# Output gates in the middle of the next chunk step, gate keys last, one rotation behind the levels

## The reference, cut to what matters

```python
def _hg_gates(hf, lb):                      # hf: forget columns, lb: learned lower bound
    logf = jnp.logaddexp(jnp.log(lb), jnp.log1p(-lb) + jax.nn.log_sigmoid(hf))
    return logf, -jnp.expm1(logf)           # log forget gate, key of the HGRN2 heads

def _merge(o_r, g_r, o_h, g_h, o_s, hg_norm_w, w_out, dtype):
    ret = _rmsnorm(o_r) * jax.nn.silu(g_r)
    hg = _rmsnorm(o_h) * hg_norm_w * jax.nn.silu(g_h)
    ...

def _post_block(x, mix, g1, b1, w_up, w_down, g2, b2):
    x = _layernorm(ALPHA * x + mix, g1, b1)
    h = jax.nn.relu(jnp.einsum('nld,df->nlf', x, w_up))
    return _layernorm(ALPHA * x + jnp.einsum('nlf,fd->nld', h * h, w_down), g2, b2)
```

## Time and profile before

| | |
|---|---|
| median of three executions | 2863.51 us |
| the profiled execution | 2869.88 us |
| its span | 2868.1 us |
| TensorE busy, share of the span | 93% |
| VectorE, ScalarE, GpSimd busy | 49%, 29%, 28% |
| mean granted TensorE clock | 0.961 of full speed |
| chunk steps of layer 0 / layer 1 | about 187 to 586 us / about 1600 to 2000 us |

### The profile page before, as it was taken

The page is one execution under the profiler, slowest core; times in us unless marked ns, Lnnn a source line. Parts: engine busy times, 40 slices in busy tenths (PEclk is TensorE's granted clock), DMA queues, the critical chain, the costliest instruction groups (busy, mean ns, idle before and its releaser), DMA issues. The chain is left out here.

```text
span 2868.1 us, 42897 instructions
## 1 busy us (share of the span) xinstructions
PE 2653.6 (93%) x17502; PEld 2408.4 (84%) x17502; DVE 1395.1 (49%) x3036; ACT 831.8 (29%) x1692; POOL 814.0 (28%) x894
## 2 busy tenths in 40 slices
PE   6998888789999999999899988787989999999996
PEld 6997776588899999999899877666889999999996
DVE  2136668556434334343741466774563434343348
ACT  2235456322121212111122445561221121212120
POOL 0027456631212111111000455664311112121110
PEclk9999989889999999999999999996999999999998
DMA  4442213162111111110344431321621111111103
GB/s 155 142 148 86 83 60 90 40 188 85 59 45 45 45 59 45 45 45 30 100 141 141 143 96 53 102 66 27 195 97 45 45 45 45 45 45 45 59 23 107
DMA packets 182357, 226.48 MB, mean 79 GB/s; under 512 B 26256, under 2 KB 158672, under 8 KB 182128
## 3 DMA queue, kind: packets, MB, share of 16 engines
q1 hardware_dynamic: 182160, 223.73, 24.2%
HBM read 182.66 MB, written 43.06 MB: 79 GB/s over the span
## 5 line engine op out<-in xcount | busy, mean ns | idle before, releaser
L950 PE MATMUL ps<-u_hi,wu_hi 128*128 128x512 f32 (+2 forms) x1536 | 498.6, 325 | 0.0
L951 PE MATMUL ps<-u_lo,wu_hi 128*128 128x512 f32 (+2 forms) x1536 | 498.0, 324 | 0.0
L952 PE MATMUL ps<-u_hi,wu_lo 128*128 128x512 f32 (+2 forms) x1536 | 495.8, 323 | 0.0
L950 PE MATMUL ps<-hid_hi,wd_hi 128*128 128x256 f32 (+2 forms) x1472 | 475.4, 323 | 17.5 <-DVE acc_a L2431 7.2
L951 PE MATMUL ps<-hid_lo,wd_hi 128*128 128x256 f32 (+2 forms) x1472 | 473.4, 322 | 0.0
L952 PE MATMUL ps<-hid_hi,wd_lo 128*128 128x256 f32 (+2 forms) x1472 | 471.9, 321 | 0.0
L2399 DVE TENSOR_TENSOR relu<-relu 128x512 f32<-128x512 f32 (+2 forms) x192 | 102.8, 535 | 531.0 <-ACT relu L1871 531.0
L950 PEld LDWEIGHTS ps<-hid_hi,wd_hi 128*128 128x128 f32 x1472 | 278.5, 189 | 39.9 <-DVE acc_a L2431 7.8
L2691 POOL TENSOR_TENSOR wd_lo<-wd_raw,wd_hi 128x1024 fp32r<-128x1024 f32 x60 | 143.2, 2409 | 589.6 <-ACT wd_hi L1846 589.6
L952 PEld LDWEIGHTS ps<-u_hi,wu_lo 128*128 128x128 f32 x1536 | 290.3, 189 | 22.0
L950 PEld LDWEIGHTS ps<-u_hi,wu_hi 128*128 128x128 f32 x1536 | 289.4, 188 | 23.0
(11 more groups left out here) (274 smaller groups left out, 5417.5 us busy)
## 6 DMA issues: line engine op xcount, KB each, us to landing
wu_raw<-in_w_up SPq DMA_DIRECT2D x32, 1024.0 KB, 5.3
wd_raw<-in_w_down SPq DMA_DIRECT2D x32, 1024.0 KB, 4.8
wl_raw<-in_w_in SPq DMA_DIRECT2D x20, 1024.0 KB, 5.3
wi_raw<-in_w_in SPq DMA_DIRECT2D x15, 1280.0 KB, 6.4
out_y<-xn SPq DMA_DIRECT2D x32, 512.0 KB, 4.3
hscr<-h_out SPq DMA_DIRECT2D x80, 160.0 KB, 1.7
hb<-hscr SPq DMA_DIRECT2D x16, 512.0 KB, 4.1
xin<-out_y SPq DMA_DIRECT2D x16, 512.0 KB, 4.1
```

What stands on the lines that cost most here:

```text
L950: nc.tensor.matmul(out, a_hi, b_hi, start=start, stop=False)
L951: nc.tensor.matmul(out, a_hi, b_lo, start=False, stop=False)
L952: return nc.tensor.matmul(out, a_lo, b_hi, start=False, stop=stop)
```

## The change

The output gates of a chunk are no longer prepared in the step before. VectorE clips them (`gates_clip(f)`) in the chunk's own step behind `front_levels(f)`, ScalarE makes their exp, ln, exp (`gates_out(f)`) behind `heads_root(h)` and place b, ahead of the exps of wave B, and VectorE multiplies (`front_silu(f)`) behind `heads_merge(h)`. GpSimd's product with hg_w (`gate_weights(f)`) moves behind the weight splits at the end of its step. The keys k0 k1 are written by `gates_keys(g)` at VectorE's end of the step, behind `heads_low(h)`, and the g_q copy of ScalarE moves from `gates_sigmoid` into `gates_log`, both with the wait for GpSimd's last level product. In step 4 GpSimd rotates chunk 5 behind `levels(4)`. The `Steps` lists follow. SyncE's and TensorE's programs stay as they are.

```diff
--- before.py
+++ after.py
@@ -491,9 +491,9 @@
         rv = Steps(sem("side_pool"), "kd v sw")
         hpe = Steps(sem("gatesT_pe"), "h")
         tpe = Steps(sem("mixT_pe"), "r q")
-        gh = Steps(sem("gates_act"), "e l r q f eg lg rg")
+        gh = Steps(sem("gates_act"), "e l r f q eg lg rg")
         ga = Steps(sem("front_act"), "kTr kTs qT eb E ka")
-        gc = Steps(sem("gates_dve"), "clip s k0 k1 f0 f1 c0 c1")
+        gc = Steps(sem("gates_dve"), "clip s f0 f1 k0 k1 c0 c1")
         gd = Steps(sem("level_dve"), "b0 b1 p ka " + " ".join(f"ar{i} al{i}" for i in levels))
         gp = Steps(sem("lev_pool"), "kst " + " ".join(f"l{i} r{i} s{i}" for i in LEVEL_ORDER) + " qe")
         rd = Steps(sem("ret_dve"), "x qi a")
@@ -1644,14 +1644,16 @@
                     nc.scalar.activation(g_r[:], g_e[:], ACT.Ln, bias=1.0).then_inc(gh.step("l"), 1)
                     act.wait_ge(gh.sem, gh.at("l", c.n))
                     nc.scalar.activation(g_r[:], g_r[:], ACT.Exp, scale=-1.0).then_inc(gh.step("r"), 1)
+
+                def gates_log(c):
+                    act.wait_ge(gc.sem, gc.at("f1", c.n))
+                    nc.scalar.activation(g_r[:], g_r[:], ACT.Ln).then_inc(gh.step("f"), 1)
                     act.wait_ge(hpe.sem, hpe.at("h", c.n))
                     act.wait_ge(gp.sem, gp.before(c.n))
                     act.wait_ge(gc.sem, gc.at("clip", c.n))
                     copy(g_q[:], ps[:, 0, 256:512].rearrange("p (a b) -> p a b", a=2)).then_inc(gh.step("q"), 1)
 
-                def gates_log(c):
-                    act.wait_ge(gc.sem, gc.at("f1", c.n))
-                    nc.scalar.activation(g_r[:], g_r[:], ACT.Ln).then_inc(gh.step("f"), 1)
+                def gates_out(c):
                     act.wait_ge(gc.sem, gc.at("c1", c.n))
                     nc.scalar.activation(gate[c.p][:], gate[c.p][:], ACT.Exp, scale=-1.0).then_inc(gh.step("eg"), 1)
                     act.wait_ge(gh.sem, gh.at("eg", c.n))
@@ -1777,6 +1779,8 @@
                     if h:
                         heads_root(h)
                     dense(step, "b")
+                    if f:
+                        gates_out(f)
                     if f and f.prompt:
                         window_exps(f, "B")
                         window_norm(f, "A")
@@ -1794,7 +1798,7 @@
                     dense(step, "e")
                     if h:
                         heads_high(h)
-                    if f and f.prompt and g:
+                    if g:
                         gates_log(g)
                     if step == 4:
                         split_wo(l, 0)
@@ -2085,15 +2089,18 @@
                     dve.wait_ge(gh.sem, gh.at("r", c.n))
                     v.tensor_tensor(g_e[:], g_e[:], g_r[:], ALU.mult).then_inc(gc.step("s"), 1)
                     dve.wait_ge(gc.sem, gc.at("s", c.n))
+                    for j in range(2):
+                        v.scalar_tensor_tensor(out=g_r[:, j, :], in0=g_e[:, j, :], scalar=lb[:, j:j + 1], in1=g_r[:, j, :],
+                                               op0=ALU.mult, op1=ALU.add).then_inc(gc.step(f"f{j}"), 1)
+
+                def gates_keys(c):
                     dve.wait_ge(gp.sem, gp.before(c.n))
                     for j in range(2):
                         v.tensor_scalar(g_k[:, j, :], g_e[:, j, :], omlb[:, j:j + 1], None, ALU.mult)\
                             .then_inc(gc.step(f"k{j}"), 1)
-                    for j in range(2):
-                        v.scalar_tensor_tensor(out=g_r[:, j, :], in0=g_e[:, j, :], scalar=lb[:, j:j + 1], in1=g_r[:, j, :],
-                                               op0=ALU.mult, op1=ALU.add).then_inc(gc.step(f"f{j}"), 1)
 
                 def gates_clip(c, h):
+                    dve.wait_ge(h_in[c.p], c.loads * 64)
                     if h:
                         dve.wait_ge(md.sem, md.at("rh", h.n))
                     for j, at in enumerate((RG, HGT)):
@@ -2333,14 +2340,13 @@
                         front_queries(f)
                     if h:
                         heads_keys(h)
-                    if f:
-                        front_silu(f)
                     if step == 0:
                         split_late(2)
                     if h:
                         heads_weights(h)
                     if f:
                         front_levels(f)
+                        gates_clip(f, chunk_at(l, step - 2))
                         if f.prompt:
                             front_masks(f, "A")
                         front_ret(f, h)
@@ -2362,22 +2368,24 @@
                         window_sums(f, "B")
                     if h:
                         heads_merge(h)
+                    if f:
+                        front_silu(f)
                     if f and f.prompt:
                         if g:
                             gates_sigmoid(g)
                         window_low(f)
-                        if g:
-                            gates_clip(g, h)
                     elif f:
                         decode_window(f)
                     if h and not h.prompt:
                         decode_states_h(h)
                     if h:
                         heads_low(h)
+                    if g:
+                        gates_keys(g)
 
                 split_late(1)
                 gates_sigmoid(chunk_at(l, 0))
-                gates_clip(chunk_at(l, 0), None)
+                gates_keys(chunk_at(l, 0))
                 v.memset(st_r[:], 0.0).then_inc(zd.step("r"), 1)
                 v.memset(st_h[:], 0.0).then_inc(zd.step("h"), 1)
                 v.memset(lev_r[:], 0.0).then_inc(zd.step("lr"), 1)
@@ -2601,8 +2609,10 @@
                     if h:
                         pool.wait_ge(mpe.sem, mpe.at("o", h.n))
                     g_.tensor_tensor(g_qe[:], g_q[:], g_eb[p][:], ALU.mult).then_inc(gp.step("qe"), 1)
-                    pool.wait_ge(gg.sem, gg.at("s1", n))
-                    hg = gate[p][:, 1].rearrange("p (h d) -> p h d", h=4)
+
+                def gate_weights(c):
+                    pool.wait_ge(gg.sem, gg.at("s1", c.n))
+                    hg = gate[c.p][:, 1].rearrange("p (h d) -> p h d", h=4)
                     g_.tensor_tensor(hg, hg, hg_w[:, :].unsqueeze(1).broadcast_to([P, 4, 64]), ALU.mult)\
                         .then_inc(rv.step("sw"), 1)
 
@@ -2651,16 +2661,20 @@
                             split_late(l, G)
                         if step in OUT_BEFORE:
                             split_wo(l, OUT_BEFORE[step])
-                    if g:
+                    if g and step != 4:
                         rotate(g)
                     if f:
                         for G in LOW_BEFORE.get(step, ())[1:]:
                             split_late(l, G)
                         levels(f, h)
+
+                        if step == 4:
+                            rotate(g)
                         for G in LOW_AFTER.get(step, ()):
                             split_late(l, G)
                         for out in OUT_AFTER.get(step, ()):
                             split_wo(l, out)
+                        gate_weights(f)
                     if h:
                         heads(h)
 
```

## The result

The changed kernel takes 2912.56 us, the median of four executions (2909.32 to 2918.91); the kernel before, beside it on the same chip, took 2863.50 (2861.42 to 2869.93). The ratio is 1.0173, with a 95% interval of 1.0153 to 1.0193: slower by 1.7%, 49 us. The forecast was 2893 with a range of 2868 to 2912. So the direction was right and the size too small, by 20 us against the median, which lies just above the range.

The account below looks back on a forecast made before the run. TensorE, busy 93% of the span, was taken to wait on VectorE's chain at step ends. Terms summed to +14.8 us a layer, +29.6 for two, making the median 2893 us, range 2868 to 2912.

Parts of the forecast that it names:

- loads of steps 0 to 2: SyncE waits for the late silu, delaying weight groups 6 and 8: +4.7 us in step 1, +4.3 in step 2, a layer.
- load of wo behind step 5: Load of wo held back by 7 to 9 us, with 8 us or more to spare: 0.
- step 7, with the lower clock: Late silu holds decode states and wo on SyncE, so ScalarE's cast waits: +8.4 us, plus 3 for lower clock, a layer.
- rotation, with the lower clock: Step 4, chunk 5 rotated behind chunk 4's levels: L1122 earlier, -4.8 us, and -2.5 for the lower clock, a layer.
- clips, silu, keys, step 8: Ends of steps 3, 5, 6 shorter, -1.5 us a layer; in step 8 silu ahead of decode probabilities, +1.7.
- the term of step 0: ScalarE's three gate activations have no idle time there; includes a group 4 load some 2 us later: +1.5 us a layer.
- The keys: Ends of steps 0 to 2: keys wait for GpSimd's weight split as clips did; otherwise each some 2.5 us shorter.
- B: Moved silu costs nothing because weights still land before ScalarE's casts; faster, 2850 us; chance 0.11.
- C: Only step 7 pays; casts of groups 6 and 8 absorb the delay; 2873 us; chance 0.08.
- D: Keys aren't shut out by GpSimd's split at the step ends; 2878 us; chance 0.07.
- E: Rotation doesn't win: step 4 gets no shorter, or the lower clock comes all the same; 2908 us; chance 0.09.
- A: The forecast itself: slower, as the terms sum; 2893 us; chance 0.65.

Follow-up runs that it names:

- mend: Changed kernel with SyncE's order altered: next hb rows (steps 0, 1, 2, 5) behind the step's loads and stores, step 7's decode states behind wo loads; 2855.05 us.
- hold: Kernel before, with only SyncE held: next hb rows in steps 1, 2, 5 and step 7's decode states also wait for the heads' merge; 2904.45 us.
- mend12: Changed kernel with SyncE's order altered in steps 0, 1 and 2 alone, next hb rows behind the step's loads; 2885.33 us.
- mend5: Changed kernel with SyncE's order altered in step 5 alone, rows of chunk 7 behind the load of wo; 2909.03 us.
- mend7: Changed kernel with SyncE's order altered in step 7 alone, silu wait and decode-state loads behind the loads of wo; 2892.12 us.
- rot: Kernel before with one part of the change alone: in step 4 GpSimd rotates chunk 5 behind the levels of chunk 4; 2855.72 us.
- gmend: Kernel before with only the gates' part of the change (clips, ScalarE chain, silu, weight product) and SyncE's order altered so no load is held; 2841.23 us.
- keys: Kernel before with one part alone: keys at the end of VectorE's step, g_q copy behind ScalarE's logarithm; 2863.42 us.
- best: Changed kernel with keys and g_q copy in their old place and SyncE's held loads reordered; 2831.02 us.

## Why the prediction was wrong, point by point

The mechanism was right: the moved silu holds SyncE, the weight groups 6 and 8 and the wo group of step 7 come late, and the steps end on ScalarE's casts. *mend* and *hold* show it from both sides. What failed are sizes. The held loads stood in the sum with 43.8 us (21 for steps 0 to 2, 0 for step 5, 22.8 for step 7) and gave back 57.5, and the rotation stood there with -14.6 and gave -9.6. The sizes, for both layers:

```
term of the sum                    predicted   measured    by
loads of steps 0 to 2              +18 (+3)    +27.2       mend12
load of wo behind step 5             0         +3.5        mend5
step 7, with the lower clock       +22.8       +20.4       mend7
rotation, with the lower clock     -14.6       -9.6        rot
all held loads together            +43.8       +57.5       mend (51.1 as three)
clips, silu, keys, step 8           +0.4       -0.7        mend against rot
```

In the first line +3 is the term of step 0, which the prediction put down mostly to ScalarE. The last line is 2 x (-1.5 + 1.7) predicted. Its measured value is the small rest between *mend* and *rot*, in which the gain of the moved gates (24.7 us by *gmend*) and the cost of the keys (24) cancel. That 57.5 - 9.6 - 0.7 = 47 comes near the 49 us of the result confirms nothing: the three are differences along one chain, from the changed kernel over *mend* and *rot* to before, and their sum is 2912.56 - 2865.34 whatever the causes are.

- **Loads of groups 6 and 8: mis-sized.** The issue was late by about what was worked out (275.1 or later predicted, 274.84 found). What failed is "it now shares the DMA engines with 1.3 MB just ahead of it; 5.5": from issue to cast the load took 7.9 us, not 5.3. L1282 of step 1 stands at 273.9 in both traces, so the cast was 7.4 us late (282.74 for 275.35) and not 5.5. Of that 0.7 us came back by the second start of L1122 (291.18 for 284.51, 6.7 late), as the prediction's 0.8 had it. Another 0.5 us was lost from there to L1282 of step 2, where the stretch at the lower clock was longer than before; the sum had no term for the clock in these steps. In all the steps grew by 7.1 and 7.0 us in layer 0 and 3.9 and 6.9 in layer 1, where 4.7 and 4.3 stood in the sum.
- **"Steps 5 and 6 hold back a load of wo by 7 to 9 us that had 8 us or more to spare: 0": wrong for step 5.** The delay against the step's L1282 was 8.3 us, as said. But counted as in step 7, 1.7 us for the three issues and 3.1 to the landing of the last, the load would take 4.8, and behind the rows of hb and the copies of the caches it took 8.6. Those 3.8 us more used up the "8 us or more to spare". In step 6, without those copies ahead of it, no cast waited, and the 0 holds.
- **Step 7: right.** Predicted 9 us of wait at the cast, about 11 at L1282 and 3 us of lower clock; found 9.33, 11.03, and L1282's products in 3.68 us instead of 1.94. *mend7* gave back 20.4 us of the 22.8.
- **The rotation: too large.** Step 4 got shorter, but of "the idle time shrinks from 6.7 us to some 1.5" 3.6 us of standing for rot_k were left in *rot*, and a part of the stretch at the lower clock with it (0.58 from 408 to 412 us). In the change itself TensorE stood 2.09 us for rot_k, the granted clock was 1.00 from 408 to 428 us, and step 4 got 7.5 and 5.0 us shorter, which is nearer to the prediction. Which of the moved instructions makes this difference to *rot* was not separated.
- **The keys: right in what they do, and too small in what they cost.** "The keys ... wait for the weight split as the clips did" is what the trace shows, 3.64 us at 286.36. Moved alone they cost nothing (*keys*), because the clips then stand ahead of them and take the wait. The prediction took the exchange as zero against before. It put an empty slot at "some 2.5 us" for each of three step ends, 15 us in all, and it is worth 24: between *mend* and *best* the steps in the first three columns differ by 1.8, 5.2 and 5.2 us in layer 0 and by 1.8, 7.5 and 3.1 in layer 1.
- **Rivals.** B is refuted by *hold*, C by *mend12* and the waits of the casts in steps 1 and 2, D by the keys' row. E was wrong in cause, though its 2908 was the nearest number: the rotation wins in each comparison. The chances hold a slip: A, D, E and most of C add up to more than the 0.82 that is written (A, D and E alone are 0.81).
- **The executions.** The forecast assumed that the changed kernel's profiled run would lie as far above its median as that of before. It lay 3.2 us below, so half of the 20 us, 9.6, is the choice of the profiled execution and none of the kernel's. By spans the miss is 10 us (39.4 against 29.6), which the loads of steps 0 to 2 (6 more), step 5 (3.5) and the rotation (5), less 2.4 at step 7, cover.

## What to carry to other kernels

Before an instruction is moved, look for a queue that waits for it and read that queue in program order: what stands behind the wait pays, and here the order of the queue alone mended it. Cost a held transfer with the traffic that is issued directly ahead of it, not with its usual time to landing. When a slot beside another engine's long instruction is cleared, as the clips' was here, its gain is lost again if an instruction of the same form is put in: leave the slot empty, or move that instruction to an engine that isn't held.

## What the hardware showed

VectorE's tensor_scalar from SBUF to SBUF stood still beside GpSimd's split (2.95 us for 0.24), while VectorE's u_lo, which reads PSUM and one tile of SBUF, took its 0.69 us inside the same split, and ScalarE's two keys took 0.71. The Trainium skill ("SBUF — State Buffer", Who interferes with whom) says that a VectorE instruction in a two-port mode, which tensor_scalar can enter, and a GpSimd instruction shut each other out. It also says that one with at most one SBUF input, outside those modes, doesn't contend, and that ScalarE waits for no one. The three rows agree; that the keys ran in such a mode is not seen in a trace.

Not expected was how long the wo weight of step 5 took. It comes in three transfers, and from the first issue to the cast that waits for it 8.6 us passed in step 5, behind rows of hb and two copies of caches, but 5.35 us in step 7, behind the decode states. An estimate from rows of before, 1.7 us for the issues and 3.1 to the last landing, gives 4.8 us, so the decode states added little. The load of group 6 landed 7.9 us after its issue, behind the rows of hb, where before it took 5.3. That the traffic ahead is the cause is read from the order of issue; no run changed it alone.
